# Wider state updates, earlier weight splits and reordered ScalarE work in a recurrent decoder layer on one Trainium2 core

## The reference

```
x += 0.5 * SwiGLU_1(RMSNorm(x))              # D_FF = 2816
h  = RMSNorm(x)
[q|f|i|g|xr|yr|gA|gB] = h @ w_in             # 1024 x 8192
# branch A, 8 heads, state 128x128 per head, in chunks of 64 tokens:
#   b = cumsum(log f) in the chunk, qe = q*exp(b), ke = k*exp(-b)
#   o = qe @ S + tril(qe ke^T) v ;  S = exp(b_last)*S + (k*exp(b_last-b))^T v
# branch B: width-4 causal conv -> r, i = sigmoid(block matmul + bias)
#   a = exp(-8 r softplus(-lambda)), h_t = a h_{t-1} + sqrt(1-a^2) i x_t ; oB = h * gelu(yr)
m  = sigmoid(gA) * (oA @ w_a_up) + sigmoid(gB) * (oB @ w_b_up)
x += m @ w_out
x += 0.5 * SwiGLU_2(RMSNorm(x)); y = RMSNorm(x)
```

## Time and profile before

| | |
|---|---|
| runs | 2703.6, 2700.48, 2702.97 us; median 2702.97 us |
| profiled execution | 2702.14 us, span 2700.2 us |
| busy of the span | PE 97%, PEld 94%, DVE 60%, ACT 41%, POOL 2% |
| chain that ended last | PE 86%, DVE 6%, ACT 4%, issue 3% |
| mean granted TensorE clock | 0.988 of full |
| HBM | 146.40 MB read, 30.23 MB written |

### The profile page before, as it was taken

How to read it: one execution, slowest core, us unless ns; L and a number is a source line. 1 busy time by engine, 2 the same in 40 slices (tenths; PEclk the granted TensorE clock), 3 DMA queues, 4 the chain that set the end, 5 groups by cost and what they waited for, 6 DMA issues and landing times.

```text
span 2700.2 us, 50133 instructions
## 1 busy us (share of the span) xinstructions
PE 2613.8 (97%) x19124; PEld 2530.0 (94%) x19124; DVE 1613.4 (60%) x2832; ACT 1095.9 (41%) x1840; POOL 60.9 (2%) x68
## 2 busy tenths in 40 slices
PE   7999999999989999999999999999999999999997
PEld 6999999999979888888899999999999999999997
DVE  5755565666586555555565766444366656565565
ACT  4332223222465555555456565311253222232334
POOL 0000000000110000000000000000100000000002
PEclk8999999999989999999999999999999999999999
DMA  2111111111121111111132213423111111111112
GB/s 107 48 55 47 47 58 50 47 47 47 58 87 56 56 54 50 55 55 55 56 110 83 81 66 147 175 100 141 40 40 48 47 47 54 47 47 54 47 51 75
DMA packets 51159, 177.86 MB, mean 66 GB/s; under 512 B 5632, under 2 KB 9984, under 8 KB 50560
## 3 DMA queue, kind: packets, MB, share of 16 engines
q1 hardware_dynamic: 51072, 176.65, 18.7%
HBM read 146.40 MB, written 30.23 MB: 65 GB/s over the span
## 4 chain that ended last, share of the span: by engine, by line
PE 86%; DVE 6%; ACT 4%; issue 3%; DMA 0%; DVEq 0%; ACTq 0%; SPq 0%; POOL 0%
PE banks L134 27%; PE banks L135 25%; PE banks L136 25%; PE banks L1288 2%; PE banks L1298 1%; PE banks L1510 1%; PE banks L1300 1%; PE banks L331 1%; PE banks L1328 1%; DVE f_blk_f L365 1%; PE banks L1279 1%; PE banks L1346 1%; DVE y L213 1%; PE banks L1334 0%; DVE f_gt L760 0%
## 5 line engine op out<-in xcount | busy, mean ns | idle before, releaser
L134 PE MATMUL banks<-f_blk_hi,f_u_hi 128*128 128x258 f32 x2496 | 711.1, 285 | 12.7 <-DVE f_blk_lo L389 12.5
L135 PE MATMUL banks<-f_blk_lo,f_u_hi 128*128 128x258 f32 x2496 | 709.7, 284 | 0.0
L136 PE MATMUL banks<-f_blk_hi,f_u_lo 128*128 128x258 f32 x2496 | 708.7, 284 | 0.0
L134 PE MATMUL banks<-mix_blk_hi,mix_u_hi 128*128 128x258 f32 x1808 | 535.3, 296 | 36.6 <-DVE sg L996 16.0
L135 PE MATMUL banks<-mix_blk_lo,mix_u_hi 128*128 128x258 f32 x1808 | 514.9, 285 | 0.0
L136 PE MATMUL banks<-mix_blk_hi,mix_u_lo 128*128 128x258 f32 x1808 | 513.8, 284 | 0.0
L134 PEld LDWEIGHTS banks<-f_blk_hi,f_u_hi 128*128 128x128 f32 x2496 | 474.8, 190 | 15.9 <-DVE f_blk_lo L389 9.3
L136 PEld LDWEIGHTS banks<-f_blk_hi,f_u_lo 128*128 128x128 f32 x2496 | 474.8, 190 | 0.0
L135 PEld LDWEIGHTS banks<-f_blk_lo,f_u_hi 128*128 128x128 f32 x2496 | 474.6, 190 | 0.1
L134 PEld LDWEIGHTS banks<-mix_blk_hi,mix_u_hi 128*128 128x128 f32 x1808 | 345.6, 191 | 63.5 <-DVE mix_u_lo L961 20.6
L135 PEld LDWEIGHTS banks<-mix_blk_lo,mix_u_hi 128*128 128x128 f32 x1808 | 345.4, 191 | 3.1 <-issue 0.2
(11 more groups left out here) (232 smaller groups left out, 3654.2 us busy)
## 6 DMA issues: line engine op xcount, KB each, us to landing
raw<-w_slabs SPq DMA_DIRECT2D x220, 512.0 KB, 3.2
sg_kept<-sgt SPq DMA_DIRECT2D x8, 1032.0 KB, 5.8
sgs<-sg_kept SPq DMA_DIRECT2D x16, 516.0 KB, 4.5
...
```

The costliest lines, as they stand in the source:

```text
L134: pe.matmul(out, wh, xh, start=start, stop=False, skip_group_check=chained)
L135: pe.matmul(out, wh, xl, start=False, stop=False, skip_group_check=chained)
L136: return pe.matmul(out, wl, xh, start=False, stop=stop, skip_group_check=chained)
```

## The change

It has these parts:

- The keys' tile `kt` becomes two tiles side by side, each 128 rows x 128, zeroed once (in group 1, on VectorE). ScalarE now makes two copies of 64 rows each, chunk 0's keys to rows 0 to 63 of the first and chunk 1's to rows 64 to 127 of the second. Both updates are matmuls over all 128 rows, and they stand one behind the other, in place of one before and one behind the output, transpose and scores. The wait of the second update for the first goes.
- Plain stage: the splits of u2 to u7 move ahead, ScalarE's among the norm's squares and VectorE's among the residual adds at the end of the first FFN. The second weight row of that stage is fetched ahead of the 4 MB store of x. The second norm's mean matmul moves from behind down product 18 to behind 21.
- HGRN groups, c = 1: ScalarE splits p6 first, ahead of square and log; the splits of the next pass's p0 and p1 move ahead of log and rstd work; VectorE makes the next pass's sums right behind p6.
- LRU groups: the merge gates' sigmoids come ahead of and right behind the Tanh; Exp and Square (`lru_power`) go to the c = 1 pass behind the split of p6; `lru_mult2` goes there too, and the sums of the next pass go ahead of the first mix.
- `load_row`: the first row of a c = 1 pass is fetched once the low parts p0 and p1 of the c = 0 pass exist.
- Up projections: the splits of the first branch's blocks (`oa_high`, `oa_low`) come behind the last mixes on VectorE; the last convolution, in two parts, and the last block's gates come one or more units later.

```diff
@@ load_row @@
     if row == 0:
-        sp.wait_ge(s.sums, four_of(j, c, 0))
+        if c:
+            sp.wait_ge(s.unit_lo, seven(j, 1, -5))
+        else:
+            sp.wait_ge(s.sums, four_of(j, 0, 0))
@@ mix_norm_scalar @@
     for m in range(KT):
         norm_square(act, k, n, 0, m)
+        if m in (1, 2, 6, 7):
+            plain_high(act, k, s, {1: 2, 2: 3, 6: 4, 7: 5}[m])
     for m in range(4):
         norm_square(act, k, n, 1, m)
+        if m < 2:
+            plain_high(act, k, s, 6 + m)
@@ mix_norm_vector @@
-        if n in (1, 2):
-            plain_low(dve, k, s, n - 1)
+        if n in (1, 2, 3, 4, 8, 9, 11, 12):
+            plain_low(dve, k, s, (1, 2, 3, 4, 8, 9, 11, 12).index(n))
@@ core_tensor @@
-    def update(n, c):
-        if c:
-            pe.wait_ge(s.u_ready, h * 18 + (2 * n + 1))
-        else:
-            pe.wait_ge(s.kt_used, h * 9 + (n + 1))
-            wait(pe, s.u_used, h * 16 + 2 * n)
-        rows = slice(c * CHUNK, (c + 1) * CHUNK)
-        pe.matmul(k.bank[6][:, c * P:(c + 1) * P], s.kt[n % 2][rows, :], s.v[rows, n, :], start=True, stop=True)\
-            .then_inc(s.u_ready, 1)
+    def updates(n):
+        pe.wait_ge(s.kt_used, h * 9 + (n + 1))
+        wait(pe, s.u_used, h * 16 + 2 * n)
+        for c in range(2):
+            pe.matmul(k.bank[6][:, c * P:(c + 1) * P], s.kt[n % 2][:, c, :], s.v[:, n, :], start=True, stop=True)\
+                .then_inc(s.u_ready, 1)
...
@@ core_scalar @@
-        act.activation(s.kt[n % 2][0:rows, :], k.bank[4][0:rows, 0:P], ACT.Copy).then_inc(s.kt_used, 1)
+        if n < 8:
+            act.activation(s.kt[n % 2][0:CHUNK, 0, :], k.bank[4][0:CHUNK, 0:P], ACT.Copy)
+            act.activation(s.kt[n % 2][CHUNK:P, 1, :], k.bank[4][CHUNK:P, 0:P], ACT.Copy).then_inc(s.kt_used, 1)
...
@@ lru_decay @@
+def lru_power(act, k, s, b):
+    wait_apart(act, s.decay, b * 3 + 1, s.act_passed)
     act.activation(s.rb[:, :], s.rb[:, :], ACT.Exp, scale=k.par[:, 3, bass.ds(b, 1)]).then_inc(s.decay, 1)
...
@@ mid_vector, head_pair @@
         pair_low(dve, k, s, j, 1, 6)
+        sums(j + 1, 0, range(4))
         cumulate(dve, k, s, j)
...
-        sums(j + 1, 0, range(4))
         finish_vector(dve, k, s, h, first)
@@ mid_vector, recurrent_pair @@
+        else:
+            lru_mult2(dve, k, s, j - 9)
+        sums(j + 1, 0, range(4), edge)
         mix(dve, k, s, j, 1, 0, s.snap_t[0][:, :])
         ahead(j + 1, 0, (0, 1), edge)
-        sums(j + 1, 0, range(4), edge)
...
@@ ups_vector @@
-    lru_conv(dve, k, s, GROUPS, range(4))
...
+        if u < 2:
+            lru_conv(dve, k, s, GROUPS, (2 * u, 2 * u + 1))
@@ build @@
-        f1 = stage("f1", FFN, first=SLAB_FFN1, norm=n1, next_norm=nm, x=k.x1, mean_after=(10, 18), **k.ffn1)
+        f1 = stage("f1", FFN, first=SLAB_FFN1, norm=n1, next_norm=nm, x=k.x1, mean_after=(10, 21), **k.ffn1)
```

More of the change, by code:

```diff
@@ L1126, in plain_scalar @@
             head_high(act, k, s, j, kappa)
-    read(0)
-    for u in (6, 7):
-        plain_high(act, k, s, u)
-    for r in range(1, 4):
+    for r in range(4):
         read(r)
@@ L1180, in plain_vector @@
                 head_low(dve, k, s, j, kappa - 1, LATE)
-    for u in (2, 3):
-        plain_low(dve, k, s, u)
     for kappa in range(KAPPAS + 1):
@@ L1202, in plain_vector @@
     affine(dve, k, s, 0, first=True)
+    pair_sums(dve, k, s, 1, 0, range(4))
     for p in (0, 1):
         pair_low(dve, k, s, 1, 0, p)
-    pair_sums(dve, k, s, 1, 0, range(4))
     cumulate(dve, k, s, 0)
@@ L1305, in core_tensor @@
     if 1 <= n < 9:
-        update(n - 1, 0)
+        updates(n - 1)
     if 2 <= n < 10:
@@ L1318, in core_tensor @@
         pe.transpose(k.bank[4][0:DEC, 0:P], s.ke[:, SEQ:T], k.ident[:, :]).then_inc(s.kt_ready, 1)
-    if 1 <= n < 9:
-        update(n - 1, 1)
     if n in (9, 10):
@@ L1327, in core_tensor @@
         pe.wait_ge(s.sc_used, h * 8 + 8)
-        pe.matmul(k.bank[6 - q][:, 0:4 * P], s.kt[0][0:DEC, :], s.vm[0:DEC, :, :], start=True, stop=True)\
+        pe.matmul(k.bank[6 - q][:, 0:4 * P], s.kt[0][0:DEC, 0, :], s.vm[0:DEC, :, :], start=True, stop=True)\
             .then_inc(s.u_ready, 1)
@@ L1376, in core_scalar @@
     if n < 9:
-        rows = P if n < 8 else DEC
         act.wait_ge(s.kt_ready, h * 9 + (n + 1))
@@ L1678, in core_pair @@
         core_turned(act, k, s, h)
+        if first:
+            act.wait_ge(s.zeroed, 5)
         for hf in range(1, 14):
@@ L1716, in lru_pair @@
         lru_gates(act, k, s, b, 2)
+        shape(j, 0, 1, s.sgt[:, 1, half(1)], ACT.Sigmoid, s.gate_shaped)
+        shape(j, 0, 0, s.sgt[:, 0, half(0)], ACT.Sigmoid, s.gate_shaped)
         lru_decay(act, k, s, b)
         pair_high(act, k, s, j, 1, 4)
-        shape(j, 0, 1, s.sgt[:, 1, half(1)], ACT.Sigmoid, s.gate_shaped)
-        shape(j, 0, 0, s.sgt[:, 0, half(0)], ACT.Sigmoid, s.gate_shaped)
+        shape(j, 0, 2, s.sgt[:, 1, half(0)], ACT.Sigmoid, s.gate_shaped)
         pair_high(act, k, s, j, 1, 5)
-        shape(j, 0, 2, s.sgt[:, 1, half(0)], ACT.Sigmoid, s.gate_shaped)
         take(j, 0, s.sgt[:, 0, half(1)], ACT.Sigmoid)
@@ L1748, in recurrent_pair @@
             finish_square(act, k, s, j - 1)
+        else:
+            lru_power(act, k, s, j - 9)
         snap(act, k, s, j, 1, 0)
+        ahead(j + 1, 0, (0, 1), edge)
         if kind == LAST_HGRN:
@@ L1754, in recurrent_pair @@
             lru_root(act, k, s, j - 9)
-        ahead(j + 1, 0, (0, 1), edge)
         snap(act, k, s, j, 1, 1)
@@ L1762, in recurrent_pair @@
             ups_high(act, k, s, 1)
-            for m in range(4):
+            for m in range(2):
                 oa_high(act, k, s, m)
@@ L1799, in core_pair @@
             dve.wait_ge(s.prod, PLAIN)
-            dve.wait_ge(s.zeroed, 3)
+            for n in range(2):
+                dve.memset(s.kt[n][:, :, :], 0.0).then_inc(s.zeroed, 1)
+            dve.wait_ge(s.zeroed, 5)
         else:
@@ L1836, in lru_pair @@
         mix(dve, k, s, j, 0, 2, s.sgt[:, 1, half(0)])
-        ahead(j, 1, (4,))
-        lru_mult2(dve, k, s, b)
-        ahead(j, 1, (5,))
+        ahead(j, 1, (4, 5))
     def head_pair(j, first):
@@ L1882, in recurrent_pair @@
             ups_low(dve, k, s, 1)
-            for m in range(2):
-                oa_low(dve, k, s, m)
         ahead(j + 1, 0, (3, 4), edge)
@@ L2040, in ups_scalar @@
     o = s.out
-    for m in (4, 5):
+    for m in range(2, KT):
         oa_high(act, k, s, m)
     ups_high(act, k, s, 2)
-    for m in (6, 7):
-        oa_high(act, k, s, m)
     ups_high(act, k, s, 3)
     for u in range(UPS):
-        if u == 1:
+        if u == 2:
             for t in range(NT):
@@ L2066, in ups_vector @@
     o = s.out
-    for m in (2, 3, 4, 5):
+    for m in range(KT):
         oa_low(dve, k, s, m)
     ups_low(dve, k, s, 2)
-    for m in (6, 7):
-        oa_low(dve, k, s, m)
     ups_low(dve, k, s, 3)
-    lru_conv(dve, k, s, GROUPS, range(4))
     for u in range(UPS):
@@ L2487, in build @@
     k.mid.el = r.put("el", [P, 24], F32)
+    k.mid.ue = [r.put(f"ue{n}", [P, 2, P], F32) for n in range(2)]
     r = Region(w1, ring.at)
@@ L2493, in build @@
     k.mid.s_out = r.put("s_out", [P, P], F32)
-    k.mid.kt = [r.put(f"kt{n}", [P, P], F32) for n in range(2)]
-    k.mid.ue = [r.put(f"ue{n}", [P, 2, P], F32) for n in range(2)]
+    k.mid.kt = [r.put(f"kt{n}", [P, 2, P], F32) for n in range(2)]
     k.mid.sgt = Region(gates_at, end).put("sgt", [P, 2, T], F32)
```

29 lines of the change are left out of this document (13 added, 16 removed).

## The result

| | before | after |
|---|---|---|
| runs (us) | 2703.6, 2700.48, 2702.97, 2703.31 | 2612.79, 2613.63, 2614.14, 2610.96 |
| median | 2703.14 | 2613.21 |
| profiled execution | 2702.14, span 2700.2 | 2612.79, span 2611.0 |
| mean granted clock | 0.988 | 0.991 |

What follows compares the result with a forecast made beforehand. TensorE, busy 97% of the span, was taken to bound the kernel. Terms 36.1 + 17.1 + 3.6 + 7.3 + 7.6 + 4.1 = 75.8 us off the profiled 2702.14 gave 2626.3, median 2627; range 2616 to 2650.

Steps and rivals of the forecast that it cites:

- Updates: Recurrence tiles on TensorE: full-row passes at 0.11 in place of 0.21 save 0.56 per tile, 36.1 us.
- HGRN groups: c = 1 passes: all seven waits of TensorE for VectorE's mix go, 17.1 us.
- Rival B: HGRN waits move, half of 17.1 + 3.6 stays, and a full pass takes 0.14: 2644 us, chance 0.15.
- rival C: In 14 groups TensorE's p3 stalls on a late weight row, slower than before: 2721 us at landing 12, chance 0.02.
- Half clock: HGRN groups: three windows of TensorE at 1.2 GHz go with the waits before them, 3 x 1.2 = 3.6 us.
- LRU groups: Seven waits for ScalarE's take go, 12.3 us; six new waits of 0.83 before p3 cost 5.0; net 7.3 us.
- Plain stage: Earlier splits and the later mean matmul remove waits of TensorE and half-clock time, 7.6 us in all.
- Up projections: Two waits and half-clock time go, a wait of 3.9 and 0.7 between blocks come: 4.1 us net.
- Rival A: Padded updates save nothing, since 0.21 per pass comes from the operands and not the rows: 2663 us, chance 0.07.

Runs made afterwards that it cites:

- updates_alone: Kernel before with only the whole edit of the updates (full rows, both side by side ahead of the output): 2648.85 us, ratio 0.9805.
- rows_only: Kernel before with both updates over all 128 rows of zero-padded key tiles, the second still behind the scores: 2657.61 us, ratio 0.9838.
- lru_undone: Changed kernel with the LRU groups' order on both engines, and group 8's c = 1 pass, as before: 2626.27 us, ratio 0.9724.

## Why the prediction was wrong, step by step

**Updates: 36.1 forecast, 49.0 measured. This is the step that failed.** I had "an entry of 0.12, four passes of 0.11 and one step of 0.11", which was right, and ended with "no row shows a full pass shorter, so no more than 36.1 is won". The bound was false, because I priced passes, taking 0.21 for each pass over 64 rows. The rows of before fit that just as well as they fit a price of 0.19 for each change of the row count, since each 64-row update stood alone there and had exactly two passes: all its steps were steps of a change. With four changes per tile the price falls on neighbours too, on the output's second pass (0.160 to 0.058) and on the way back to the product (0.202 + 0.225 to 0.031 + 0.201), and I had left these as they were. 64 tiles x (0.77 - 0.56) is the 13 us that are missing. The earlier trace rows had the sign: the output's four passes take 0.49 there, where four steps of 0.112 make no more than 0.45.

The rule stood in the Trainium skill, "TensorEngine Tiling (Array Packing)", Key Properties: changing the tiling mode, and not merely the tile, drains TensorE. It gives no price; the runs here give 0.19 us for each change, at 64, 32 and 8 rows, and none at 96. That TensorE drains is the page's word; the traces show only the two longer steps. I had looked up that page's other section, which recommends row tiling for a contraction of 64, and weighed only that.

**HGRN groups: 17.1 forecast, 17.3 measured** (2.47 in each of seven). Timeline after, c = 1 of group 2 as in the earlier trace rows, two rows of ScalarE and four of VectorE:

```profile
905.60 0.60 ACT L1671 ACTIVATE q<-banks 128x516 f32<-128x516 f32 x1
906.09 0.62 ACT L959 ACTIVATE mix_u_hi<-mix_sum 128x512 fp32r<-128x512 f32 x1
...
909.43 0.69 DVE L985 TENSOR_TENSOR mix_sum<-raw 128x512 f32<-128x512 f32 x1 [1.99 <-DMA raw<-w_slabs]
...
912.04 2.28 DVE L1237 TENSOR_TENSOR_SCAN b<-reset,b 128x1024 f32<-128x1024 bf16 x1
914.24 0.67 DVE L999 TENSOR_TENSOR vb<-banks,mix_snap 128x516 f32<-128x516 f32 x1
...
923.26 0.69 DVE L999 TENSOR_TENSOR sg<-banks,mix_snap 128x516 f32<-128x516 f32 x1
```

With P = 905.57 the sums begin at P + 3.9 (forecast 3.2), the mix into `vb` ends at P + 9.3 (8.8) and the mix for p6 at P + 18.4 (17.7), ahead of P + 18.9. Every step came 0.5 to 0.7 late, through the weight row, and the mix for p6 used 0.7 of the 1.2 to spare. Rival B had this place right and its size wrong; of rival C nothing was seen.

**Half clock.** I had three windows and 3.6; the groups that had one before are 1.4 to 1.5 us shorter than the others, 4.4 in all, and one behind the up projections, at the start of the second FFN, went too. But the reason that I gave, windows follow the waits, is only half shown: updates_alone kept every wait for `sg` and had one window in groups 1 to 7 instead of three, rows_only had three in other groups, and the four executions of lru_undone differ by 8.6 us. Fewer waits went with fewer windows over all kernels here (mean clock 0.988 to 0.990 before, 0.991 to 0.993 after), but a single window can't be forecast.

**LRU groups: 7.3 forecast, 5.3 measured** between before and after (6.4 by lru_undone). Timeline after, group 12: the take and Square on ScalarE, `lru_mult2` and, behind the four sums, the mix on VectorE, TensorE:

```profile
1442.70 0.60 ACT L1671 ACTIVATE sgt<-banks 128x516 f32<-128x516 f32 x1 [0.91 <-PE banks L136]
...
1446.40 1.07 ACT L1541 ACTIVATE z<-rb 128x1032 f32<-128x1032 f32 x1
...
1447.50 1.23 DVE L1587 SCALAR_TENSOR_TENSOR tb<-z,tb 128x1032 f32<-128x1032 f32 x1 [2.96 <-ACT z L1541]
...
1451.18 0.69 DVE L999 TENSOR_TENSOR mix_snap<-banks,mix_snap 128x516 f32<-128x516 f32 x1
...
1452.01 0.36 PE L134 MATMUL banks<-mix_blk_hi,mix_u_hi 128*128 128x258 f32 x1 [0.73 <-DVE mix_snap L999]
```

The mechanism is the forecast one, and its price too: 0.83 was forecast, 0.81 to 0.87 measured. What I missed is group 8, whose c = 1 pass has the same new order and nothing to win by it: 0.9 is lost there, and lru_undone gives it back. Groups 9 to 14 gained 0.97 each. Group 15, which has no new wait, should have gained 1.76 and gained some 0.4: the wait for `h_f` behind it is 3.7 where lru_undone has 2.4, so 1.3 of it came back as a longer wait for that DMA.

**Plain stage: 7.6 forecast, 7.0 measured**, of which 1.6 returned in group 1 as a wait I hadn't named. **Up projections: 4.1 forecast, 5.2 measured** (of the 5.6 of group 15 and this stage 0.4 belong to the LRU order): the wait for `h_f` was 3.7 against 3.9, and the 0.7 between blocks is the row of `h_lo`.

The sum by the traces is 49.0 + 17.3 + 4.4 + 5.3 + 7.0 + 5.2 = 88.2. Start-up, the window in the second FFN's first product and the final norm make next to nothing together, and 89.4 lie between the profiled executions; the 1.2 left over are ahead of the first product, behind the last and in roundings. Without the first term 39.7 were forecast and 39.2 measured. Rival A is refuted by rows_only.
